# First norm of a two-block transformer kernel: scale and shift loaded in pairs by chunk, shifts multiplied on TensorE, constants behind

## What is computed

```python
mod = (silu(c) @ w_ada[0] + b_ada[0])[:, None, :]          # w_ada: 1024 x 6144
shift1, scale1, gate1, shift2, scale2, gate2 = split(mod, 6)
h = rmsnorm(x) * g_pre_mix[0] * (1 + scale1) + shift1
y = h @ w_in[0]                                            # then the mixers read y
```

## Time and profile before

| | |
|---|---|
| median of 3 runs | 3341.17 us (3339.67 to 3341.28) |
| the profiled execution | 3341.82 us, of which its span is 3340.0 us |
| TensorE (PE) busy | 96% of the span |
| VectorE (DVE) busy | 74% |
| ScalarE (ACT) busy | 53% |
| mean granted TensorE clock | 0.978 of full speed |

### The profile page before, as it was taken

One profiled execution on the slowest core, in us unless ns is written; L12 is line 12 of the kernel. 1 busy time (PEld: TensorE's weight loads), 2 busy tenths in 40 slices (PEclk: granted clock), 3 DMA queues, 4 the chain that ended last, 5 costly groups with the idle time before them and its releaser, 6 DMA issues.

```text
span 3340.0 us, 64435 instructions
## 1 busy us (share of the span) xinstructions
PE 3190.1 (96%) x27178; PEld 3100.9 (93%) x27178; DVE 2465.2 (74%) x3750; ACT 1757.9 (53%) x2676; POOL 3.0 (0%) x6
## 2 busy tenths in 40 slices
PE   6899999989999999989999999999999999998999
PEld 6789899989989999879999989999978999997999
DVE  8987699887767676787676667667667667678766
ACT  4556444555544454575454546455456455456544
POOL 0000000000000000000000000000000000000000
PEclk8899999989999999999999999999999999999999
DMA  8455488444546655535555644555543555552453
GB/s 310 143 175 193 148 315 315 154 133 149 177 144 218 200 164 189 166 105 178 188 184 186 188 139 165 188 188 184 189 152 130 189 186 186 187 174 97 165 188 131
DMA packets 164351, 597.93 MB, mean 179 GB/s; under 512 B 18240, under 2 KB 18272, under 8 KB 163936
## 3 DMA queue, kind: packets, MB, share of 16 engines
q1 hardware_dynamic: 164064, 593.81, 53.5%
HBM read 592.69 MB, written 1.05 MB: 178 GB/s over the span
## 4 chain that ended last, share of the span: by engine, by line
PE 77%; DVE 15%; ACT 5%; issue 2%; DMA 1%; SPq 0%; DVEq 0%; ACTq 0%
PE ps L476 25%; PE ps L478 24%; PE ps L477 24%; DVE wlo L436 4%; DVE fa L1541 2%; ACT whi L424 2%; DVE land L551 1%; DVE fa L2434 0%; DMA land<-w_ada 0%; DMA land<-w_in 0%; DVE h L1789 0%; PE ps L1130 0%; DVE tmps L855 0%; DVE tmps L584 0%; PE ps L2286 0%
## 5 line engine op out<-in xcount | busy, mean ns | idle before, releaser
L476 PE MATMUL ps<-h,whi 128*128 128x256 f32 x5472 | 1546.6, 283 | 34.9 <-DVE h L750 19.8
L477 PE MATMUL ps<-h,whi 128*128 128x256 f32 x5472 | 1535.6, 281 | 0.0
L478 PE MATMUL ps<-h,wlo 128*128 128x256 f32 x5472 | 1535.4, 281 | 0.0
L436 DVE TENSOR_TENSOR wlo<-land,whi 128x1024 fp32r<-128x1024 f32 (+1 forms) x1032 | 1218.7, 1217 | 258.5 <-ACT whi L424 257.5
L424 ACT ACTIVATE whi<-land 128x1024 fp32r<-128x1024 f32 (+1 forms) x1032 | 1028.7, 1044 | 146.2 <-PE ps L478 132.9
L476 PEld LDWEIGHTS ps<-h,whi 128*128 128x128 f32 x5472 | 1037.0, 190 | 43.5 <-issue 30.1
L477 PEld LDWEIGHTS ps<-h,whi 128*128 128x128 f32 x5472 | 1037.1, 190 | 0.8
L478 PEld LDWEIGHTS ps<-h,wlo 128*128 128x128 f32 x5472 | 1036.7, 189 | 0.0
L477 PE MATMUL ps<-y,whi 128*128 128x256 f32 x1472 | 410.9, 279 | 0.0
L476 PE MATMUL ps<-y,whi 128*128 128x256 f32 x1472 | 410.9, 279 | 0.0
L478 PE MATMUL ps<-y,wlo 128*128 128x256 f32 x1472 | 410.9, 279 | 0.0
(11 more groups left out here) (444 smaller groups left out, 2829.6 us busy)
## 6 DMA issues: line engine op xcount, KB each, us to landing
land<-w_gu SPq DMA_DIRECT2D x352, 512.0 KB, 3.5
land<-w_dn SPq DMA_DIRECT2D x176, 512.0 KB, 3.5
land<-w_in SPq DMA_DIRECT2D x136, 512.0 KB, 3.9
land<-w_ada SPq DMA_DIRECT2D x96, 512.0 KB, 3.9
land<-w_up SPq DMA_DIRECT2D x88, 512.0 KB, 4.1
land<-hg_in SPq DMA_DIRECT2D x64, 512.0 KB, 3.5
land<-w_down SPq DMA_DIRECT2D x44, 512.0 KB, 4.4
land<-ple_gate SPq DMA_DIRECT2D x32, 512.0 KB, 3.6
```

Of the source, the lines that this page charges most:

```text
L436: dve.tensor_tensor(w.lo, g.slot(n), w.hi.bitcast(F32), ALU.subtract).then_inc(*D_("w_lo", n))
L476: pe.matmul(out, w.hi, x.hi, start=first, stop=False, skip_group_check=skip)
L477: pe.matmul(out, w.hi, x.lo, start=False, stop=False, skip_group_check=skip)
L478: return pe.matmul(out, w.lo, x.hi, start=False, stop=last, skip_group_check=skip)
```

## The change

- **Tiles.** The scale tiles `w_ada` 8 to 15 stay as they were. The shift tiles 0 to 7 are replaced by eight tiles `w_shift` with the same numbers the other way round, and TensorE multiplies them (`shift_tensor`: 8 float32 matmuls of a 128 x 128 block and one column of silu(c)). Shifts 0 and 1 are multiplied behind the squares; shift k + 1 is multiplied in `lead_tensor` ahead of chunk k, for k from 1 to 6.
- **Chunks.** Gain, shift and normed chunk are made chunk by chunk (`first_norm_scalar`, `first_norm_vector`). VectorE handles `w_ada` 9 + k between x times gain of chunk k and the low part of chunk k. `lead_tensor` takes two projections (four tiles) in the first layer too.
- **Order of loads.** 130 columns of parameters (65 KB) and 257 of constants (129 KB), x, two tiles of `w_in`, scale 0 and shift 0, two more of `w_in`, the other seven pairs, tiles 4 and 5 of `w_in`, the rest of the parameters (375 KB) and constants (663 KB), the positions, then the list as before. Modulation tiles 16 to 39 ride from tile 6 of `w_in` on.
- **Slots.** The four lead tiles keep slots 5 to 8; the sixteen others take turns in the other seven. Slot by slot this gives: the loads of shift 3, shift 4, shift 5, shift 6 and shift 7 wait for scales 0, 1, 2, 3 and 4, those of scales 4 to 7 for shifts 0 to 3, tile 4 of `w_in` for scale 7, and tile 5 for shift 7.
- **Waits.** TensorE waits for the rest of the constants behind `lead_tensor`; VectorE waits for it ahead of halving the taps of the convolution; ScalarE waits for it at `lam`. `ya_apply` waits for one more tile.

```diff
+    def place(self):
+
+        self.index = {(name, i): n for n, (name, i, kind) in enumerate(self.order)}
+        self.part, self.ring, self.emptied, held, count = {}, {}, {}, {}, 0
+        keep, cycle = [5, 6, 7, 8], [9, 10, 0, 1, 2, 3, 4]
+        for n, (name, i, kind) in enumerate(self.order):
+            if kind not in ("split", "mod", "shift"):
+                continue
             if kind == "split":
                 self.part[n] = len(self.part)
...
+            if count >= 20:
+                slot = count % self.NL
+            elif kind == "split":
+                slot = keep.pop(0)
+            else:
+                slot = cycle[0]
+                cycle = cycle[1:] + cycle[:1]
+            if slot in held:
+                self.emptied[n] = held[slot]
+            self.ring[n] = slot
+            held[slot], count = n, count + 1
+        self.split = list(self.part)
...
-    sp.dma_start(g.par[:, :], g.args["params"]).then_inc(*D_("params", by=16))
+    early = PARAM_COLS["early"]
+    sp.dma_start(g.par[:, 0:early], g.args["params"][:, 0:early]).then_inc(*D_("params", by=16))
     for n, (name, i, kind) in enumerate(g.order):
         if kind == "consts":
-            sp.dma_start(g.con[:, :], g.args["consts"]).then_inc(*D_("consts", by=16))
+            a = CONST_COLS["early"]
+            sp.dma_start(g.con[:, 0:a], g.args["consts"][:, 0:a]).then_inc(*D_("consts", by=16))
+        elif kind == "more":
+            a = CONST_COLS["early"]
+            sp.dma_start(g.par[:, early:NPAR], g.args["params"][:, early:NPAR]).then_inc(*D_("more_params", by=16))
+            sp.dma_start(g.con[:, a:NCON], g.args["consts"][:, a:NCON]).then_inc(*D_("more_consts", by=16))
...
+            if n in g.emptied:
+                before = g.emptied[n]
                 if before in g.part:
                     sp.wait_ge(*W("tile", before))
                 else:
-                    sp.wait_ge(*W("ada", g.order[before][1]))
-            sp.dma_start(g.slot(n), g.args[name][i]).then_inc(*D_(f"landed{r % g.NL}", n, by=16))
...
-def lead_tensor(g, pe, projections, x, ready):
+def lead_tensor(g, pe, projections, x, ready, shifts=False):
...
     for k in range(8):
+        if shifts and 0 < k < 7:
+            shift_tensor(g, pe, k + 1)
         pe.wait_ge(*W(*ready[k]))
         for n, i, out in parts:
             mm = mm3(pe, out, g.weights(n)[:, k * 128:(k + 1) * 128], x.chunk(k), k + i == 0, k == 7, skip=True)
...
-        if i == 0:
+        if i == 8:
...
-        if i % 8 == 7:
+        if i % 8 == 7 and i > 15:
...
+    act.preload_act_table_set(NORM_TABLE)
     act.wait_ge(*W("params"))
     act.activation(g.small[:, 570:578], g.par[:, c:c + 8], ACT.Exp, scale=-1.0).then_inc(*D_("c_exp"))
-    act.wait_ge(*W("consts"))
+    row_scalar(g, act)
+
+
+def more_scalar(g, act):
+
+    D_, W = g.m.done, g.m.when
+    act.wait_ge(*W("more_params"))
+    act.wait_ge(*W("more_consts"))
     act.activation(g.causal[:, 0:128], g.C("ident", 0, 128), ACT.Copy)
     act.activation(g.causal[:, 128:256], g.C("mask", 0, 128), ACT.Copy).then_inc(*D_("causal"))
-    row_scalar(g, act)
+
+
+def first_norm_scalar(g, act):
+
+    D_, W = g.m.done, g.m.when
+    A, base, xr = g.small[:, 560:568], g.small[:, 578:586], g.fa1[:, 0:2048]
+    squares_scalar(g, act, "m0")
+    split_scalar(g, act, 2)
+    rough_scalar(g, act, ("m0",), ("sumsq", "m0"), g.t(8)[:, 0:T])
+    for k in range(9):
+        if k:
+            act.wait_ge(*W("shift", k - 1))
+            act.wait_ge(*W("normed", "m0", k - 1))
+            act.activation(g.h.chunk(k - 1).hi, xk(xr, k - 1), ACT.Identity, bias=g.mod[:, k - 1:k]).then_inc(
+                *D_("h_hi", "m0", k - 1))
+        if k < 8:
+            act.wait_ge(*W("base_gain"))
+            act.wait_ge(*W("ada", 8 + k))
+            act.activation(A[:, k:k + 1], g.mod[:, 8 + k:9 + k], ACT.Identity, scale=g.P("g_pre_mix", k),
+                           bias=base[:, k:k + 1]).then_inc(*D_("chunk_gain", k))
+            act.wait_ge(*W("shift_sum", k))
+            act.activation(g.mod[:, k:k + 1], g.ps[5 + k % 2][:, k:k + 1], ACT.Identity, bias=g.P("b_ada", k)).then_inc(
+                *D_("shift", k))
+        if k == 0:
+            split_scalar(g, act, 4)
+    split_scalar(g, act, 6)
...
-    a = PARAM_COLS["cf_conv"]
+    b, gc = PARAM_COLS["b_ada"] + 8, PARAM_COLS["g_pre_mix"]
     dve.wait_ge(*W("params"))
-    dve.tensor_scalar(g.par[:, a:a + 248], g.par[:, a:a + 248], 0.5, None, ALU.mult).then_inc(*D_("cf_taps"))
+    dve.scalar_tensor_tensor(g.small[:, 578:586], g.par[:, b:b + 8], 1.0, g.par[:, gc:gc + 8], ALU.add, ALU.mult).then_inc(
+        *D_("base_gain"))
     dve.wait_ge(*W("c_exp"))
...
+def first_norm_vector(g, dve):
+
+    D_, W = g.m.done, g.m.when
+    A, r, xr = g.small[:, 560:568], g.small[:, T:2 * T], g.fa1[:, 0:2048]
+    split_vector(g, dve, 1)
+    var_vector(g, dve, "m0")
+    rsqrt_vector(g, dve, ("m0",), r, g.small[:, 0:T], g.t(8)[:, 0:T], g.t(8)[:, T:2 * T])
+    split_vector(g, dve, 2)
+    modulation_vector(g, dve, g.index["w_ada", 8] + 1)
+    dve.wait_ge(*W("x_in"))
+    dve.wait_ge(*W("factor", "m0"))
+    for k in range(8):
+        dve.wait_ge(*W("chunk_gain", k))
+        dve.scalar_tensor_tensor(xk(xr, k), xk(g.x, k), A[:, k:k + 1], r, ALU.mult, ALU.mult).then_inc(
+            *D_("normed", "m0", k))
+        if k == 0:
+            split_vector(g, dve, 4)
+        if k < 7:
+            modulation_vector(g, dve, g.index["w_ada", 9 + k] + 1)
+        h = g.h.chunk(k)
+        dve.wait_ge(*W("h_hi", "m0", k))
+        dve.scalar_tensor_tensor(h.lo, xk(xr, k), g.mod[:, k:k + 1], h.hi.bitcast(F32), ALU.add, ALU.subtract).then_inc(
+            *D_("h", "m0", k))
+    split_vector(g, dve, 6)
+    a = PARAM_COLS["cf_conv"]
+    dve.wait_ge(*W("more_params"))
+    dve.wait_ge(*W("more_consts"))
+    dve.tensor_scalar(g.par[:, a:a + 248], g.par[:, a:a + 248], 0.5, None, ALU.mult).then_inc(*D_("cf_taps"))
...
+    for k in range(2):
+        shift_tensor(g, pe, k)
+
+
+def shift_tensor(g, pe, k):
+
+    D_, W = g.m.done, g.m.when
+    n, bank = g.index["w_shift", k], 5 + k % 2
+    w = g.slot(n)
+    pe.wait_ge(*landed(g, n))
+    pe.wait_ge(*W(*g.banks.use(bank, "shift", k)))
+    for c in range(8):
+        mm = pe.matmul(g.ps[bank][:, k:k + 1], w[:, c * 128:(c + 1) * 128], g.sc[:, c:c + 1], start=c == 0, stop=c == 7)
+    mm.then_inc(*D_("shift_sum", k))
...
-    lead = [s for s in MIX if s[0] in PROJECTIONS][:2 if lay else 1]
+    lead = [s for s in MIX if s[0] in PROJECTIONS][:2]
     for step, i, bank in MIX:
         ps = g.ps[bank] if bank is not None else None
         if (step, i, bank) == lead[0]:
-            lead_tensor(g, pe, [mix_projection(st, lay, *s) for s in lead], g.h, chunks("h", st))
+            lead_tensor(g, pe, [mix_projection(st, lay, *s) for s in lead], g.h, chunks("h", st), lay == 0)
+            if lay == 0:
+                pe.wait_ge(*W("more_consts"))
...
+            if lay == 0:
+                more_scalar(g, act)
...
+            act.wait_ge(*W("tile", g.index[BRANCH[2], lay * 4 + 3]))
...
-    out.append(("consts", 0, "consts"))
-    out.extend(("w_ada", i, "mod") for i in range(16))
-    out.insert(7, ("xT", 0, "xT"))
-    out.append(("positions", 0, "positions"))
...
+        if lay == 0:
+            lead, rest = out[first:first + 4], out[first + 4:]
+            out[first:] = [("consts", 0, "consts"), ("xT", 0, "xT"), *lead[:2], ("w_ada", 8, "mod"), ("w_shift", 0, "shift"),
+                           *lead[2:]]
+            for k in range(1, 8):
+                out.extend([("w_ada", 8 + k, "mod"), ("w_shift", k, "shift")])
+            out.extend([*rest[:2], ("more", 0, "more"), ("positions", 0, "positions")])
+            first = len(out)
+            out.extend(rest[2:])
```

More of the change, by code:

```diff
@@ L28, in _plan_params @@
     at = 0
-    for name, n in [("c", 8), ("g_pre_mix", 16), ("b_ada", 96), ("lam", 8), ("da_g_subln", 2),
+    for name, n in [("c", 8), ("g_pre_mix", 16), ("b_ada", 96), ("lam", 8), ("da_g_subln", 2), ("early", 0),
                     ("mla_g_cq", 6), ("mla_g_ckv", 4), ("sc_conv", 24), ("cf_conv", 248),
@@ L47, in _plan_consts @@
     at = 0
-    for name, n in [("ident", 128), ("ones", 128), ("islope", 16), ("qscale", 8), ("room", 104), ("mask", 128), ("dist3", 384),
-                    ("maskT", 128), ("lev", 192), ("rot", 96), ("inv", 1), ("rst", 256), ("eps", 1), ("spare", 14)]:
+    for name, n in [("ident", 128), ("ones", 128), ("eps", 1), ("early", 0), ("islope", 16), ("qscale", 8), ("room", 104), ("mask", 128), ("dist3", 384),
+                    ("maskT", 128), ("lev", 192), ("rot", 96), ("inv", 1), ("rst", 256), ("spare", 14)]:
         CONST_COLS[name] = at
@@ L326, in __init__ @@
         self.ps = [self.bank[:, i * 512:(i + 1) * 512] for i in range(8)]
-        self.part, self.ring = {}, {}
-        for n, (name, i, kind) in enumerate(order):
+        self.place()
+        self.rewind()
+    def place(self):
```

(38 more changed lines are left out.)

8 lines of the change are left out of this document (2 added, 6 removed).

## The result

The changed kernel takes 3349.08 us (median of 7 executions, 3346.17 to 3353.65) where the kernel before took 3339.67 beside it (7 executions, 3338.04 to 3341.28). The ratio is 1.0028 [1.0018, 1.0037]: slower, by 9.4 us. I had forecast 3363.7, so the direction was right and the size more than twice too large. The profiled execution took 3349.15 us, of which the span is 3347.4, against 3341.82 of the kernel before: 7.3 more.

The account below looks back on a forecast made before the run. VectorE's place in its program was taken to set the time: shift 7 at 61.2 plus 12.2 us of loads puts the first tap at 73.4 instead of 50.86, 22.5 us later, hence 3363.7 us; range 3346 to 3368.

Parts of the forecast that it names:

- The sum of squares: Start of the kernel: the sums of squares end at 15.0 us, a time called S.
- The first chunk: Norm ahead of the lead: chunk 0 ready at S + 10.2, so TensorE starts its lead at 25.2 us.
- TensorE per chunk: Lead: twelve matmuls 2.6 us at low clock or 1.4 at high, plus a shift of 3.4 or 1.9.
- Both bounds of the one-column price: Shift at clock 0.50: at least 1.4 us if weight loads ignore the clock, at most 3.4; 3.4 taken.
- The loads behind the lead: From shift 7 to the first tap: tile 5, constants, tiles 6 and 7 and their splitting take 12.2 us.
- Nothing takes it back: From first tap to the wait at the reduction: VectorE has no idle time, so the 22.5 us delay stays.
- Which clock: Lead: clock 0.50 throughout, 6.0 us a chunk, so shift 7 at 61.2 us.
- rival 1: Lead: clock rises at 28.9 us, first tap at 58.9, 8.0 us later than before, total 3349.2; chance 0.15.
- the values between them: Between forecast and rival 1: a swinging clock or cheaper one-column load at 0.50, the latter giving 3351.7; chance 0.12.
- No change: Whole kernel: 3338 to 3347 us, rival 1 with a shift at its lower bound and early S; chance 0.06.
- an early S: Sums of squares ending before the assumed 15.0 us; all at full clock would give 12.7.
- Faster: Lead: VectorE sets the pace, norm ends at 39.2, total 3336, if a shift costs under 0.6 us; chance 0.07.

Follow-up runs that it names:

- the repeat: The changed kernel run once more with the same code: 3349.04 us, ratio 1.0026 to the kernel before.
- warm: Changed kernel plus four unread dense matmuls behind shift 0 and nine behind shift 1, filling TensorE's idle time: 3344.88 us, 1.0013.
- best2: Changed kernel with slots reordered, shift 2 ahead of the lead, earlier splits of tiles 4 and 5, and 8, 3, 1 dense matmuls behind shifts 0 to 2: 3336.51 us.

## Why the prediction was right in direction and wrong in size

**Held.** *The sum of squares* ended at 14.97 (9.03 + 5.94), with 15.0 forecast. *The first chunk* was ready at 25.1 (24.61 + 0.48), with 25.2 forecast. *TensorE per chunk* was sized right at both clocks: a shift of 3.41 us at 0.50 (3.4) and 1.84 at 1.00 (1.9), twelve matmuls 2.56 (27.94 + 3.41 = 31.35 to 33.91) and 1.35. Both bounds of the one-column price had been open; the reading that such a pair costs its weight load, and that the load follows the clock, gave the right price (sixteen weight loads of a shift in the repeat: 3.53 us at 0.50, 1.87 at 1.00). *The loads behind the lead* took 12.5 us from the end of shift 7 (48.6) to the first tap (61.10), with 12.2 forecast, with TensorE in the wait for constants that was named (3.6 us). *Nothing takes it back* held up to the wait at the reduction: 10.2 us at the first tap, 9.9 at the reduction. Behind it the prediction took the stages to be the same whenever they start. The profiled execution ends only 7.3 us later than that of the kernel before, the medians lie 9.4 apart; whether those 2.5 us are the spread between executions or come from the later start is open.

**Failed: "Which clock".** That step took 0.50 for the whole lead, by the row of 146 to 152.9 us, and so shift 7 at 61.2. The clock rose at 34.1 in the profiled execution (39.3, 40.6 and 40.0 in three other profiles with the same lead), and from there a round took 3.19 us instead of 6.0. The working of the step can be followed to the result: rival 1 had the rise at 28.9 and shift 7 at 46.7; a rise 5.2 us later costs 5.2 x 0.47 = 2.4, hence 49.1, measured 48.6. Then 48.6 + 12.5 is the 61.10. Rival 1, to which I had given 0.15, is thus what happened, at 3349.2 forecast against 3349.08, partly by luck: it had the first tap 2.2 us too early (58.9), and its sum started from a median of before of 3341.17, 1.5 above the one measured beside the change. The run with one projection shows that the forecast's condition exists: with half the dense matmuls the clock did stay low for the whole lead.

The row I chose was the wrong neighbour. Its stretch had TensorE busy for 6.9 us, while a lead of six rounds is some 20 us at least; a row can say that the clock had not risen after 6.9 us and no more. The next two stretches of the same trace were there to be read:

```profile
152.90:156.30 3.40, 3.40 (x17) 3.40 (x17) 3.23 (x11) 2.36 (x10) 0.00 (x0) 0.50 0.00 0
...
156.40:231.50 75.10, 69.88 (x571) 68.28 (x570) 62.61 (x103) 44.29 (x65) 0.00 (x0) 1.00 0.60 201
```

TensorE went on without a gap, now with matmuls of 256 columns, and the clock rose near 156.3 us, 10.3 us after the start of my row. Where a round costs 6.0 us in one state and 3.3 in the other and no row reaches as far as the lead is long, the moment of the rise is itself an unknown with two ends (28.9 and never), and the values between them, to which I gave 0.12, deserved more; I took one end. What decides the moment stays open: the runs bound it and don't explain it.

On the rule that I weighed there: the Trainium skill (TensorE: Matmul & The Clock Gate, "What's actually happening") says that activity releases the throttle. For this kernel that was the better guide to the end state, since the gapless lead did get the high clock. Yet its plain reading would have the rise come as early as without the shifts, and it came 9 to 16 us into the lead instead of 3.0 to 3.9 (first loads alone, kernel before, shifts on VectorE); and the lead with one projection, 31.4 us without a gap, didn't get it at all.

**The other rivals.** *No change* wanted a shift at 1.4 us and an early S; neither came. *Faster* wanted shifts that fit in TensorE's idle time; 1.84 us against the 0.6 that decides. The runs add what neither rival had: even at the high clock throughout (warm: 56.83) the change costs 6 us at the first tap, and only with the slot order, a shift taken out of the lead's rounds and earlier splits as well does it come out ahead.

## What to carry to other kernels

Before moving small matmuls into a lead, price them in both states of the clock and compare that with what the engine they leave needs per round: here 3.19 us against 3.08 at best, 5.97 at worst. Follow each buffer slot that such a step now holds, for a queue in program order passes the delay on to everything behind it (4 of the 9 us here). And test the parts of a change apart: the first loads alone gave 1.5 us at the first tap and 3.2 in the median, at the edge of the noise, so the rest cost some 11 to 12 (9.4 and those).

## What I had not expected of the hardware

- The clock rose late, but it rose, in a gapless stretch in which 16 of 28 matmuls have a single column (9 to 15.5 us after its start, in four profiles); with 16 of 22 it stayed at 0.50 through 31.4 us without a gap. Halving the one-column matmuls (8 of 20) brought it no sooner (16 us).
- When it rose differed by 5.2 us between two executions of the same kernel (34.1 and 39.3), and by 6.5 among four profiles of the same lead (34.1 to 40.6).
- Once at 1.00 it stayed there through the same rounds (warm, best2), and also with TensorE idle 1.4 us in each round of 3.08 (shifts on VectorE). Dense matmuls that nobody reads, put into a gap ahead, bought about 4 us.
- A one-column float32 matmul stands in the trace as two pairs of weight load and matmul, and these follow the clock: 3.41 us for 16 pairs at 0.50 (0.213 each) and 1.84 at 1.00 (0.115). That is about the price of a matmul of 256 columns in the same rounds (2.56 and 1.35 us for twelve, 0.213 and 0.113 each).
